# Two orders of the split matmuls in a streamed GEMM: high, high, low, low against high, low, high, low

## What is computed

```
# first block
for layer in range(2):
    hn = rmsnorm(h, norm_w[layer])
    h = h + (hybrid_layer(hn, ...) if layer == 0 else shortconv_layer(hn, ...))
#   hybrid_layer:    proj = h @ w_in; gated delta rule, dilated attention; concat @ w_out
#   shortconv_layer: split(h @ w_in, 4); short convolution, gates; @ w_out
x = rmsnorm(h, final_norm_w)

# second block
h = rms_norm(x, norm_mix_g) * (1 + sc1) + sh1
u, q, k, v, ga, gb = split(h @ w_in)
merged = sigmoid(ga) * (s5_branch(u) @ w_proj_ssm) + sigmoid(gb) * (moba_attention(q, k, v) @ w_proj_attn)
x = x + g1 * (merged @ w_out)
h2 = rms_norm(x, norm_mlp_g) * (1 + sc2) + sh2
x = x + g2 * (square(relu(h2 @ w_ff1)) @ w_ff2)
return rms_norm(x, norm_final_g)
```

## Time and profile before

| | us |
|---|---|
| median of three runs | 3021.09 |
| lowest, highest | 3020.56, 3025.32 |
| the profiled execution | 3025.32 |
| its span | 3023.3 |
| TensorE matmul busy | 2953.2 (98%) |
| TensorE weight load busy | 2572.6 (85%) |
| VectorE busy | 2152.5 (71%) |
| ScalarE busy | 1506.3 (50%) |
| GpSimd busy | 452.1 (15%) |

### The profile page before, as it was taken

The page is one execution under the profiler, slowest core; times in us unless marked ns, Lnnn a source line. Parts: engine busy times, 40 slices in busy tenths (PEclk is TensorE's granted clock), DMA queues, the critical chain, the costliest instruction groups (busy, mean ns, idle before and its releaser), DMA issues.

```text
span 3023.3 us, 51503 instructions
## 1 busy us (share of the span) xinstructions
PE 2953.2 (98%) x17546; PEld 2572.6 (85%) x17546; DVE 2152.5 (71%) x3020; ACT 1506.3 (50%) x2164; POOL 452.1 (15%) x187
## 2 busy tenths in 40 slices
PE   7999999999999999999998999999999999999998
PEld 6889898889987888888887877788887888888887
DVE  6666666676568888888877899876687426565465
ACT  4454444544444444444444777766544444444443
POOL 0111011110100000000000000000002445545443
PEclk9999999999999999999998999999999999999999
DMA  6444434444457887888885545456785566766655
GB/s 214 143 138 132 136 131 142 139 139 146 147 192 254 311 298 282 317 303 303 301 294 172 166 168 168 166 194 211 246 303 172 188 210 223 243 236 236 206 182 174
DMA packets 172690, 629.41 MB, mean 208 GB/s; under 512 B 19224, under 2 KB 20376, under 8 KB 171808
## 3 DMA queue, kind: packets, MB, share of 16 engines
q1 hardware_dynamic: 165024, 601.99, 57.6%
q10 hardware_dynamic: 7552, 25.91, 2.5%
HBM read 615.22 MB, written 12.60 MB: 208 GB/s over the span
## 4 chain that ended last, share of the span: by engine, by line
PE 69%; issue 24%; DVE 4%; ACT 2%; DMA 1%; DVEq 0%; POOL 0%; SPq 0%; ACTq 0%; POOLq 0%
PE gemm L537 42%; PE gemm L542 21%; PE side L670 1%; PE side L677 1%; DVE wl L1520 1%; ACT wh L976 1%; PE side L682 1%; PE side L563 0%; DMA raw<-in_stream 0%; DMA x<-in_x 0%; PE side L737 0%; DVE gB L1711 0%; ACT gA L1078 0%; DVE xs L1599 0%; PE side L714 0%
## 5 line engine op out<-in xcount | busy, mean ns | idle before, releaser
L537 PE MATMUL gemm<-xs,wh 128*128 128x512 f32 x5120 | 1649.6, 404 | 28.7 <-DVE xs L1599 8.6
L976 ACT ACTIVATE wh<-raw 128x1024 fp32r<-128x1024 f32 x939 | 984.4, 1058 | 925.9 <-PE gemm L542 799.6
L1520 DVE TENSOR_TENSOR wl<-raw,wh 128x1024 fp32r<-128x1024 f32 x811 | 1035.7, 1281 | 451.2 <-ACT wh L976 428.7
L542 PEld LDWEIGHTS gemm<-xs,wl 128*128 128x128 f32 x5120 | 967.1, 189 | 229.4
L542 PE MATMUL gemm<-xs,wl 128*128 128x256 f32 x5120 | 1013.2, 279 | 0.0
L537 PEld LDWEIGHTS gemm<-xs,wh 128*128 128x128 f32 x5120 | 786.4, 190 | 56.5 <-issue 50.8
L537 PE MATMUL gemm<-hid,wh 128*128 128x512 f32 x2368 | 748.5, 397 | 6.7 <-DVE fxg L1525 2.2
L542 PEld LDWEIGHTS gemm<-hid,wl 128*128 128x128 f32 x2368 | 446.8, 189 | 102.0
L542 PE MATMUL gemm<-hid,wl 128*128 128x256 f32 x2368 | 468.8, 279 | 0.0
L1449 POOL TENSOR_TENSOR wl<-raw,wh 128x1024 fp32r<-128x1024 f32 x128 | 348.8, 2730 | 370.5 <-ACT wh L976 370.5
L537 PEld LDWEIGHTS gemm<-hid,wh 128*128 128x128 f32 x2368 | 358.4, 189 | 9.7 <-ACT wh L976 3.3
(11 more groups left out here) (377 smaller groups left out, 1951.4 us busy)
## 6 DMA issues: line engine op xcount, KB each, us to landing
raw<-in_stream SPq DMA_DIRECT2D x940, 512.0 KB, 3.8
ada_a<-in_ada SPq DMA_DIRECT2D x144, 512.0 KB, 5.0
ada_b<-in_ada SPq DMA_DIRECT2D x48, 512.0 KB, 5.1
stash<-stage ACTq DMA_DIRECT2D x12, 512.0 KB, 3.0
att<-stash ACTq DMA_DIRECT2D x8, 384.0 KB, 4.0
x<-in_x SPq DMA_DIRECT2D x4, 512.0 KB, 5.7
xacc<-in_x ACTq DMA_DIRECT2D x1, 2048.0 KB, 11.2
stash<-stA ACTq DMA_DIRECT2D x4, 512.0 KB, 6.5
```

What stands on the lines that cost most here:

```text
L537: mm(G[n][:, :], wh[:, slot, at:at + P], rhs(sl * SLAB_K + k), start=sl == 0 and k == 0, stop=False, skip_group_check=True)
L542: op = mm(G[n][:, T:2 * T], wl[:, slot, at:at + P], rhs(sl * SLAB_K + k)[:, 0:T], start=False, stop=last, skip_group_check=True)
L976: A(wh[:, slot, :], raw[:, slot, :], ACT.Copy).then_inc(hi_ready, 1)
L1520: tt(wl[:, slot, :], raw[:, slot, :], wh[:, slot, :].bitcast(F32), ALU.subtract).then_inc(lo_ready[slot], 1)
```

## The change

Inside a set of four, the two loops over `k` become one. The high and the low matmul of block 0 are issued one after the other, then those of block 1. Operands, shapes, output regions, the flags of the first and the last matmul and all waits and signals stay where they were: `start` is on the first matmul of a bank, `stop` and the signals on the last.

```
@@ -533,14 +533,14 @@
                     if sl == 0:
                         wait(pe, bank_freed, 4 * g + n - 3)
                     for k in range(SLAB_K):
+                        xk = rhs(sl * SLAB_K + k)
                         at = (k * SLAB_N + n) * P
-                        mm(G[n][:, :], wh[:, slot, at:at + P], rhs(sl * SLAB_K + k), start=sl == 0 and k == 0,
-                           stop=False, skip_group_check=True)
-                    for k in range(SLAB_K):
-                        at = (k * SLAB_N + n) * P
+                        first = sl == 0 and k == 0
                         last = sl == nslabs - 1 and k == SLAB_K - 1
-                        op = mm(G[n][:, T:2 * T], wl[:, slot, at:at + P], rhs(sl * SLAB_K + k)[:, 0:T], start=False,
-                                stop=last, skip_group_check=True)
+                        mm(G[n][:, :], wh[:, slot, at:at + P], xk, start=first, stop=False,
+                           skip_group_check=True)
+                        op = mm(G[n][:, T:2 * T], wl[:, slot, at:at + P], xk[:, 0:T], start=False, stop=last,
+                                skip_group_check=True)
                     if n == SLAB_N - 1:
                         op.then_inc(slab_used, 1)
                     elif sl == nslabs - 1:
```

## The result

The changed kernel takes 3044.89 us, the median of four runs between 3042.79 and 3049.26, against 3021.24 us for the kernel before. The medians lie 23.65 us apart. The ratio, worked out over all executions on record, is 1.0074, with a 95% interval of 1.0061 to 1.0085; that is 22 us. The forecast was no change, 3021 us, in a range that ended at 3040.

The account below looks back on a forecast made before the run. The prediction took TensorE's back-to-back matmuls to bound the kernel. Four terms of 0 us each left the median of 3021.1 us at 3021 us, with an 8-in-10 range of 3003 to 3040 us.

Parts of the forecast that it names:

- What bounds the kernel: TensorE, busy 98%; 3744 sets take about 2602 us, and each nanosecond per set is worth 3.7 us.
- Term 1, streaming: Columns per set stay 1536 and half the columns cost half the time, so 0 us.
- Term 2, weight loads: Each matmul covers one load; two loads under high and two under low matmuls before and after, so 0 us.
- Term 3, neighbours: Steps between high and low matmuls in a set, four instead of two: taken as 0, ends -37 and +37 us.
- its upper part: The slower rival's larger form, up to 0.01 us per set from neighbours, 3040 to 3058 us: chance 0.04.
- The hint I leaned on: 16 alike 512-column matmuls take 0.229 us each, against 0.230 to 0.235 for a high matmul in a set.
- Term 4, restarts: After a wait the first load lies bare; a set starts with a high matmul before and after, so 0 us.
- The slower one: High-to-low steps wait for columns just written; 0.0025 us per set, 9 us, around 3030 us: chance 0.26.
- The first faster one: The `xs` sets come down to the 0.693 us of `hid`, saving 8 to 9 us, 3012 us: chance 0.17.
- The opposite shift for `hid`: The 1184 `hid` sets slow by the same size as `xs` would gain: only 4 us, under what can be told.

Follow-up runs that it names:

- old_wh_apart: Kernel before, tiles reordered so wh alone starts at an even multiple of 64 bytes, wl, xs and hid at odd ones: 3062.14 us, ratio 1.0132.
- old_xs_moved: Kernel before with xs placed behind the small tiles, at an odd multiple of 64 bytes like hid: 3019.06 us, ratio 0.9987.
- low_left: Changed kernel, but the low matmul adds into the left 256 columns of the bank instead of the right: 3043.59 us, ratio 1.0065.
- old_wl_apart: Kernel before, tiles reordered so wl alone starts at an even multiple of 64 bytes, wh, xs and hid at odd ones: 3041.10 us, ratio 1.0062.
- new_xs_plus32: Changed kernel with xs 32 bytes further and hid unmoved: 3028.86 us, ratio 1.0025 to the kernel before.

## Why the prediction was wrong

**What bounds the kernel** held. TensorE sets the time, the sets make up most of it, and a nanosecond per set is worth about 3.7 us. By the paces of the table, over 2560 sets with `xs` and 1184 with `hid`, an undisturbed set went from 695.9 to 703.9 ns. These 8.0 ns would be 30 us; 27 appeared in the short distances and 9 came back in the longer ones. I had not counted on anything coming back.

**Term 1, streaming,** was 0 by an argument that could not carry it. Half the columns for half the time was read from the two-digit starts, and it told only that no large fixed price exists.

**Term 2, weight loads,** was 0 because each load has a cover before and after. The cover is there after too. But the place of the weight tiles changes the pace of the old order by up to 2.8% (693.5 to 712.7 ns with `xs`), with the loads still under the matmuls. Counting covers was the wrong question. The Trainium skill (TensorE: Matmul & The Clock Gate, Part 2) says that loading the next weights takes no read bandwidth from the running matmul, as the two have ports of their own. The runs do not show what happens at the ports, and whether the load or the matmul is held is open. They do not agree that the place of the weights costs nothing: with the same instructions, old_wh_apart took 3062 us and old_xs_moved 3019, and of the tiles that the sets read only `wl` has moved.

**Term 3, neighbours,** is the step that failed: the exchange of steps between shapes was put at 0 and measures 0.0080 us per set, 5.8 ns with `xs` (15 us) and 12.9 with `hid` (15 us). I wrote that it was known to 0.01 us per set, took 0, and kept 37 us as the end. The bound was right, and the range still stopped at 3040, because I gave its upper part only 0.04.

The trace of before held more than two digits show. In ns, over about 1000 undisturbed steps of each kind with `hid`, high to high takes 226.3, high to low 235.6, low to low 118.4 and low to high 113.5; the prediction read 0.23 for both of the first two. With `xs` they are 233.0, 233.3, 115.0 and 116.2. Trading one high-to-high and one low-to-low step for one high-to-low and one low-to-high costs 4.4 ns by these with `hid` and 1.5 with `xs`, 9 us in all: the right sign, and a third of what came. The rest is that the steps do not keep their price. In the changed kernel with `hid`, high to low takes 234.8 ns, but low to high 118.4. The hint I leaned on, that 16 alike matmuls cost about what one in a set costs, tells nothing about an alternating order: the pace belongs to the whole repeating sequence in its layout, not to a step.

**Term 4, restarts,** was right as to their price. But after a restart what follows with `xs` can run at another pace, and that I had not seen: in the trace of before one pace per operand was enough.

**The rivals.** The slower one had the right sign, and with `hid` the signs that it named (high to low at 0.235 or more, no shorter low to high) came true; but its cause is wrong, as low_left shows, and its price of 0.0025 us was a guess, a third of the 0.0080 measured. The first faster one named what mattered, how the reads of weights and columns fall together, and took 693 ns with `hid` for a merit of `hid`'s place. It was a merit of that place in that order. In the new order the same place is the bad one, 706.6. The opposite shift for `hid` had been put at 3 ns and 4 us, as too small to tell; it was 12.9 ns, half of the loss.

What is shown: the pace hangs on the sequence of shapes and on the place of both weight tiles relative to the moving operand. What stays open is why. Over stretches of 24 matmuls most sets lie at 680, 693.3, 696.7, 700, 706.7 or 713.3 ns, all of them whole multiples of 3.33 ns apart, and I have no run that shows where that grid comes from, nor what picks one of two paces after a late start.

## What to carry to other kernels

Where one engine issues without a gap, read its pace in ns over a long undisturbed stretch for each operand by itself. If the same instructions run at two paces, suspect the addresses, and test a new order in more than one layout before judging it: here the alternating order was 0.7% slower in one layout and 0.14% faster than the kernel before in another. Two digits of a timeline cannot clear a change that touches 3744 sets.

## What I had not expected of the hardware

- The same sequence of 512- and 256-column matmuls at the same addresses can run at two paces, each kept for tens of us: 693.3 or 706.7 ns a set for the alternating order, 700 or 706.7 for the old order in old_wl_apart.
- Moving one weight tile and the small tiles in SBUF, with the same instructions, moved the time of the old order from 3019 to 3062 us.
- A shift of the moving operand by 32 bytes took away the slow one of its two paces (new_xs_plus32, 693.3 ns).
